# Three transfers instead of one for two weight loads near the end of an expert stream

## What is computed

```python
z = xb @ w_up[e] + b_up[e]
x_glu = jnp.minimum(z[:, ::2], SWIGLU_LIMIT)
x_lin = jnp.clip(z[:, 1::2], -SWIGLU_LIMIT, SWIGLU_LIMIT)
y = x_glu * jax.nn.sigmoid(SWIGLU_ALPHA * x_glu) * (x_lin + 1.0)
return y @ w_down[e] + b_down[e]
```

## Time and profile before

| what | value |
|---|---|
| median of 3 runs | 1134.8 us |
| the profiled execution's own time | 1134.97 us |
| its span, first to last instruction | 1133.2 us |
| granted TensorE clock, mean | 0.999 |
| PE busy | 1103.4 us, 97% |
| DVE, ACT, GpSimd (POOL) busy | 28%, 20%, 3% |
| moved by the transfer engines | 437.99 MB, mean 387 GB/s |
| queue of SP (q1) | 91.7% of 16 engines |

### The profile page before, as it was taken

The page is one execution under the profiler, slowest core; times in us unless marked ns, Lnnn a source line. Parts: engine busy times, 40 slices in busy tenths (PEclk is TensorE's granted clock), DMA queues, the critical chain, the costliest instruction groups (busy, mean ns, idle before and its releaser), DMA issues.

```text
span 1133.2 us, 14624 instructions
## 1 busy us (share of the span) xinstructions
PE 1103.4 (97%) x5774; PEld 491.7 (43%) x5774; DVE 313.6 (28%) x794; ACT 228.7 (20%) x635; POOL 34.6 (3%) x71
## 2 busy tenths in 40 slices
PE   9999999999999999999999999999999999999997
PEld 6788878844243333333433333333332323233322
DVE  6565662122212121213221313030303021212123
ACT  3663454412020101010101010111110101010103
POOL 1200012200000000000000000000000000000000
PEclk9999999999999999999999999999999999999999
DMA  9743528999999999999999999999999999999995
GB/s 349 292 162 116 166 105 341 408 397 421 429 427 430 436 427 430 433 429 431 422 426 434 427 431 436 428 430 437 428 430 436 429 430 436 429 426 428 427 423 235
DMA packets 31263, 437.99 MB, mean 387 GB/s; under 512 B 5616, under 2 KB 7944, under 8 KB 10360
## 3 DMA queue, kind: packets, MB, share of 16 engines
q1 hardware_dynamic: 30592, 435.64, 91.7%
q10 hardware_dynamic: 624, 1.68, 0.4%
HBM read 436.00 MB, written 2.41 MB: 387 GB/s over the span
## 4 chain that ended last, share of the span: by engine, by line
PE 73%; DMA 22%; DVE 2%; issue 1%; ACT 1%; SPq 0%; DVEq 0%
PE bank L1407 26%; DMA ring<-in_experts 21%; PE bank L1445 16%; PE bank L1113 10%; PE bank L1159 5%; PE bank L1303 4%; PE bank L1282 3%; PE bank L1227 1%; PE bank L1316 1%; PE bank L1306 1%; DVE area L1861 1%; PE bank L1279 1%; PE bank L984 1%; PE bank L995 1%; DMA ring<-in_opening 1%
## 5 line engine op out<-in xcount | busy, mean ns | idle before, releaser
L1407 PE MATMUL bank<-ring,area 128*64 128x512 f32 x1872 | 424.7, 597 | 7.3 <-DMA ring<-in_experts 6.9
L1407 PEld LDWEIGHTS bank<-ring,area 128*64 128x64 f32 x1872 | 126.6, 136 | 276.2 <-issue 254.0
L1445 PE MATMUL bank<-ring,area 128*64 128x512 f32 x960 | 220.6, 599 | 5.9 <-DMA ring<-in_experts 5.8
L1849 DVE TENSOR_TENSOR x_tok<-x_tok,bank 128x512 f32<-128x512 f32 x60 | 41.3, 688 | 326.6 <-PE bank L1303 326.6
L862 ACT ACTIVATE area<-area 128x256 f32<-128x256 f32 x64 | 26.7, 417 | 513.7 <-DVE area L1861 513.7
L1113 PE MATMUL bank<-ring 128*128 128x264 f32 (+1 forms) x512 | 119.6, 391 | 0.0
L1445 PEld LDWEIGHTS bank<-ring,area 128*64 128x64 f32 x960 | 63.5, 136 | 122.8 <-issue 107.2
L1113 PEld LDWEIGHTS bank<-ring 128*128 128x128 f32 x512 | 95.8, 190 | 20.0 <-issue 1.3
L1886 DVE TENSOR_TENSOR area<-area 128x1024 f32<-128x1024 f32 x15 | 18.4, 1225 | 209.5 <-ACT area L872 209.5
L1303 PE MATMUL bank<-area 128*128 128x512 f32 x128 | 71.8, 644 | 0.0
L1159 PE MATMUL bank<-area,ring 128*128 128x264 f32 x256 | 58.6, 387 | 0.0
(11 more groups left out here) (292 smaller groups left out, 685.6 us busy)
## 6 DMA issues: line engine op xcount, KB each, us to landing
ring<-in_experts SPq DMA_DIRECT2D x64, 4096.0 KB, 24.9
ring<-in_experts SPq DMA_DIRECT2D x36, 2048.0 KB, 30.4
ring<-in_experts SPq DMA_DIRECT2D x24, 1024.0 KB, 9.0
ring<-in_w_in SPq DMA_DIRECT2D x16, 1024.0 KB, 9.5
area<-in_experts SPq DMA_DIRECT2D x7, 2048.0 KB, 13.1
area<-in_experts SPq DMA_DIRECT2D x3, 4096.0 KB, 20.8
ring<-in_w_out SPq DMA_DIRECT2D x8, 1024.0 KB, 4.8
area<-in_experts SPq DMA_DIRECT2D x4, 1024.0 KB, 8.3
```

Source lines behind the costliest of these rows:

```text
L1407: m = mm(bank[2 * h + n][64 * e:64 * e + 64, :], xe[:, k, 64 * e:64 * e + 64], w[:, kk, e, NB * n:NB * (n + 1)], start=False, stop=(k == K ...
L1445: m = mm(bank[4 + c][64 * e:64 * e + 64, :], y_t[:, 4 * half + f, 64 * e:64 * e + 64], w[:, f, e, :], start=False, stop=(half == 1 and f = ...
L1849: eng.tensor_tensor(x, x, combined_bank(unit, last)[:, :], ALU.add).then_inc(s.added, 1)
```

## The change

Loads 185 and 186 are issued as three transfers each instead of one. The first has partitions 0 to 111, the second partitions 112 to 119, the third partitions 120 to 127; all have the whole 16 KB of their rows. By the change's own description the two transfers of eight rows are shared by only the eight lowest-numbered transfer engines. `signals` tells PE to count 3 x 16 for these loads. The bytes, their places in SBUF and the order of the loads stay.

```diff
+SHARED = (185, 186)
+EVEN_ROWS, FEW_ROWS = 112, 8
...
-    return 3 if n == WIDE + 1 else 2 if WIDE <= n <= WIDE + HALVED else 1
+    return 3 if n == WIDE + 1 or n in SHARED else 2 if WIDE <= n <= WIDE + HALVED else 1
...
+            def shared_dma(n, dst, full):
+
+                for lo in (0, *range(EVEN_ROWS, P, FEW_ROWS)):
+                    rows = slice(lo, EVEN_ROWS if lo == 0 else lo + FEW_ROWS)
+                    eng.dma_start(dst[rows, :], source(n)[rows, :]).then_inc(full, 16)
...
                 eng.wait_ge(s.ring_used, n - RING + 1)
-                if i <= UP_LOADS:
+                if n in SHARED:
+                    shared_dma(n, dst, full)
+                elif i <= UP_LOADS:
                     expert_dma(n, dst, full)
```

## The result

The change makes the kernel slower: 1152.76 us, median of 4 runs from 1152.36 to 1155.47, against 1134.89; the ratio is 1.0162 with an interval from 1.0149 to 1.0175. That is +17.9 us where +3.8 was forecast. The span grew from 1133.2 to 1150.7 us.

The account below looks back on a forecast made before the run. Landing of load 188 was taken to bound the end; lower engines lose 2.45 us per load, +4.9 for two, of which 2.7 to 4.9 reaches PE; middle +3.8 on 1134.8 gives 1138.6 us, range 1134.0 to 1143.0 (8 in 10).

Parts of the forecast that it names:

- What bounds the kernel: At the kernel's end: landing of load 188 plus work no longer waiting; queue delays above some 0.5 us reach the end.
- The 112-row transfer: Loads 185 and 186: 4.28 us at usual pace, 8.6 at the 32-row stretch's pace; taken as 4.90, like a whole load.
- The spread of the engines: Last loads: engines finish over 3.5 us, so small transfers don't meet fully; factor 2, 2.45 us for two per load.
- The row of the biases: Bias loads of 32 rows, from 117.0 to 118.8 us: engines busy at 1.05 and 1.03, moving only 208 and 205 GB/s.
- Rival 6: Loads 185 and 186: an eight-row transfer goes over one engine alone; +18 us, 1153 us; chance 2%.
- Rival 1: Loads 185 and 186: rows cost the same, lower eight engines finish first, 2.2 us ahead; -1.0 us, 1133.8 us; chance 12%.
- Rival 2: Loads 185 and 186: rows cost the same, but a lower engine is among the last; +1.2 us, 1136.0 us; chance 10%.
- Rivals 3 and 5: Small transfers: contention mild or hidden, some 1135.8 us, chance 15%; or they come together, some 1143.7 us, chance 11%.
- The clock: Whole kernel: no other engine sees the change and the clock stays at 1.00, so it adds nothing.

## Why the prediction was wrong, point by point

**What bounds the kernel** was right. The landings of the last loads set the end, a delay of the queue passes on, and three transfers cost nothing as such.

**The 112-row transfer** is the step that failed: "I take one row time on top: 4.90 us, as a whole load before". With it and equal shares the kernel is 14.4 us slower, and the forecast had +0 for this part. Alone it takes 6.74 us, halfway to the upper bound of 8.6 that I had written down; in the stream an added one costs 12.5, above both. But no bound held the other half, and that is the premise behind all terms of the sum: that a transfer changes its own rows' time, and the engines that are still in the load ahead or already in the one behind go on at their pace. They don't. Once some engines are in the odd rows, all 16 deliver half, until the last is out: 212 GB/s over 26 us, with each of the 73 rows at 1.16 us or more. The engines stand 4.1 us apart, so the stretch is longer than the transfer; that this makes the 6 us that a group of such loads pays once fits, but no run varies the spread.

**The spread of the engines** I read the wrong way round. I took it as the reason why the small transfers wouldn't meet, and chose a factor of 2 for them. With engines in different loads at a time, the small ones meet the ordinary ones instead. Four small ones cost 9.9 us added alone; my working has 4 x 1.22 = 4.9. In the change, where they stand in a stretch that is at half pace anyway, they and the uneven share add 3.5 us to the 14.4.

**The row of the biases** said it: 208 GB/s with the engines at 1.05. I used it for the small transfers and not for the 112 rows, because 112 looked near to 128. How near doesn't count: 64 rows cost nothing in one arrangement and 14.3 us for two loads in the other. What counts is how the partitions lie.

**Rival 6** names 1153 us, which was measured, by a wrong way: eight rows over one engine. The packets show eight completions, and eight rows alone took 1.40 us where one engine would take 4.9. **Rival 1** is out: with four more rows for eight engines, and no row slowed, the kernel is 1.9 us slower (0.7 to 2.7), and the spread of load 188 is 6.7 us, so the eight aren't the first eight. **Rival 2** had that right, that one of them is among the last, and was wrong in that rows cost the same. **Rivals 3 and 5** share the failed premise. The blocks of four were weighed for the small transfers alone; with 7 rows for each engine, rows 0 to 111 can't be laid out in blocks of four either.

**The clock** was taken to stay at 1.00. It fell to 0.50 behind PE's waits; it costs 2.02 us on load 186, of which some 1.0 reaches the end.

**Open** is why ordinary loads slow down all together, and not only those engines whose partitions are written by another. That engines queue behind each other on the way in is an argument, not shown. Also open is which partitions each engine gets in a transfer of 112 or 64 rows, and which engines are the late ones. So it isn't settled whether an engine is slow because it meets another one, or because it is away from the partitions that it writes in a load of 128 rows: no run in the stream separates the two.

## What to carry to other kernels

In a stream that keeps all transfer engines busy, keep every transfer at 128 partitions and cut along the columns; where rows must be cut, every second partition cost nothing here, and blocks of 64 or of 112 and 16 cost 14 us for two loads. Before an odd transfer is put into such a stream, price it there, not alone: one load as 112 and 16 rows costs 3.6 us by its shapes alone and 10.4 in the stream. To undo the spread of the engines by shares is worth at most 2.0 us here, by which the last completion of load 188 is behind the mean of the 16, and the way to do it cost 18.

## What the hardware did that I had not expected

- A block of partitions as destination halves the rate of all 16 engines: 188 to 213 GB/s at a busy share of 0.96 to 1.04, where 425 to 431 is usual. Two transfers of eight rows are enough (+5.0 us for each pair, 0.26 MB). All rows of 16 KB in that stretch, those of ordinary loads too, take 0.83 to 1.94 us instead of 0.61.
- With 64 alternate partitions the stream keeps its 431 GB/s, with 64 neighbouring ones it falls to 188; the source's rows make no difference (+5.1 against +18.8 us).
- One group of loads as 112 and 16 rows costs some 6 us, and each load 4.3 us on top.
- The 16 engines don't finish a load together: their completions lie over 4.1 us in the steady stream, and over 5.7 to 10 us once transfers of eight rows have gone through.
- A busy share near 1.00 says nothing about the rate: only the GB/s beside it does.
